# Routed expert layers gathered from group 0 alone, with later pairs shifted, a scatter signalled bank by bank, and another evacuation order in the attentions

## What is computed

```python
def hier_moe(h, w_grp, b_grp, w_exp, b_exp, w_gate, w_up, w_down):   # 4 groups of 8 experts, hidden 256
    pg = softmax(t @ w_grp + b_grp);  p_top, grp = lax.top_k(pg, 1)
    le_sel = (einsum('td,gde->tge', t, w_exp) + b_exp)[arange(T), grp[:, 0]]
    val, idx = lax.top_k(le_sel, 2)
    wts = softmax(val) * p_top
    ...
    a = silu(einsum('td,edh->teh', t, w_gate)) * einsum('td,edh->teh', t, w_up)
    y = sum over experts of (a * combine) @ w_down
```

## Time and profile before

| | |
|---|---|
| runs | 2247.03, 2251.01, 2254.46 (median 2251.01) |
| profiled execution | 2245.17, of which the span is 2243.4 |
| TensorE matmul busy | 1813.4 (81%), 13243 instructions |
| VectorE, ScalarE busy | 431.5 (19%), 396.5 (18%) |
| chain that ended last | PE 57%, DMA 33%, DVE 4%, ACT 2% |
| transfers | 716.11 MB, mean 319 GB/s |

### The profile page before, as it was taken

One profiled execution on the slowest core, in us unless ns is written; L12 is line 12 of the kernel. 1 busy time (PEld: TensorE's weight loads), 2 busy tenths in 40 slices (PEclk: granted clock), 3 DMA queues, 4 the chain that ended last, 5 costly groups with the idle time before them and its releaser, 6 DMA issues.

```text
span 2243.4 us, 30956 instructions
## 1 busy us (share of the span) xinstructions
PE 1813.4 (81%) x13243; PEld 1125.3 (50%) x13243; DVE 431.5 (19%) x1014; ACT 396.5 (18%) x898; POOL 0.6 (0%) x5
## 2 busy tenths in 40 slices
PE   7989899999898998899987556566789976656556
PEld 5858565568676655587754122211577542212113
DVE  2242211123533111223311000000244210000001
ACT  3030211122532111222321000000213310000001
POOL 0000000000000000000000000000000000000000
PEclk9999899999799999999998887877999987777778
DMA  9876799975536999933579999999942799999993
GB/s 358 255 256 251 290 389 392 392 230 185 210 152 236 360 398 397 346 125 130 187 298 413 421 422 421 421 422 421 346 141 101 298 414 421 421 421 421 421 421 163
DMA packets 184735, 716.11 MB, mean 319 GB/s; under 512 B 28396, under 2 KB 95896, under 8 KB 114072
## 3 DMA queue, kind: packets, MB, share of 16 engines
q1 hardware_dynamic: 183884, 713.61, 81.5%
q10 hardware_dynamic: 716, 0.53, 0.1%
HBM read 826.30 MB, written 1.05 MB: 369 GB/s over the span
## 4 chain that ended last, share of the span: by engine, by line
PE 57%; DMA 33%; DVE 4%; ACT 2%; SPq 2%; issue 1%; ACTq 0%; POOLq 0%; DVEq 0%
DMA ring<-in_w 27%; PE ps L986 19%; PE ps L1416 7%; PE ps L1339 7%; DMA ring<-in_moe_w_up 6%; PE ps L1349 3%; PE ps L1428 3%; PE ps L1366 2%; PE ps L1323 2%; PE ps L963 2%; PE ps L1140 2%; SPq L808 1%; PE ps L1000 1%; PE ps L1053 1%; PE ps L1041 1%
## 5 line engine op out<-in xcount | busy, mean ns | idle before, releaser
L1416 PE MATMUL ps<-ring,ptb 128*32 128x512 f32 x1936 | 316.8, 804 | 201.5 <-DMA ring<-in_w 188.0
L1416 PEld LDWEIGHTS ps<-ring,ptb 128*32 128x32 f32 x1936 | 83.5, 141 | 422.4 <-issue 407.3
L1428 PE MATMUL ps<-ring,pb 128*32 128x512 f32 x1024 | 155.3, 765 | 88.0 <-DMA ring<-in_w 85.3
L986 PE MATMUL ps<-xT,ring 128*128 128x256 f32 (+2 forms) x640 | 146.7, 388 | 1.0 <-ACT xT L1720 0.4
L1428 PEld LDWEIGHTS ps<-ring,pb 128*32 128x32 f32 x1024 | 40.8, 136 | 195.8 <-issue 191.8
L986 PEld LDWEIGHTS ps<-xT,ring 128*128 128x128 f32 (+2 forms) x640 | 117.7, 187 | 29.4 <-issue 8.4
L986 PE MATMUL ps<-oT,ring 128*128 128x256 f32 x512 | 114.0, 381 | 2.0 <-DVE oT L2228 1.1
L2457 DVE TENSOR_TENSOR kT<-pb,ps 128x1024 f32<-128x1024 f32 x8 | 9.8, 1221 | 531.6 <-ACT pb L1894 531.6
L986 PE MATMUL ps<-hT,ring 128*128 128x256 f32 x480 | 106.7, 380 | 1.5 <-ACT hT L1720 1.5
L1339 PE MATMUL ps<-ring,vt 128*32 128x256 f32 x1536 | 93.5, 400 | 16.1 <-DMA ring<-in_moe_w_up 15.6
L986 PEld LDWEIGHTS ps<-oT,ring 128*128 128x128 f32 x512 | 96.2, 190 | 15.6 <-DVE oT L2228 2.0
(11 more groups left out here) (437 smaller groups left out, 1955.2 us busy)
## 6 DMA issues: line engine op xcount, KB each, us to landing
ring<-in_w SPq DMA_DIRECT2D x370, 1024.0 KB
ring<-in_moe_w_gate SPq DMA_DIRECT2D x96, 1024.0 KB
ring<-in_moe_w_up SPq DMA_DIRECT2D x96, 1024.0 KB
ring<-in_moe_w_down SPq DMA_DIRECT2D x96, 1024.0 KB
ring<-in_ada_w SPq DMA_DIRECT2D x48, 1024.0 KB
ring<-in_diff_w_in SPq DMA_DIRECT2D x12, 1024.0 KB
ring<-in_w_o SPq DMA_DIRECT2D x8, 1024.0 KB
ring<-in_ple_gate_w SPq DMA_DIRECT2D x8, 1024.0 KB
```

The lines of the kernel that those rows point to most:

```text
L986: last = mmul(o, l, r, start=start, stop=stop)
L1416: last = mmul(ps[32 * j:32 * j + 32, 2 * a + h, :], xg[:, k, 32 * j:32 * j + 32], w[j][2 * k2 + h], start=(k == 0), stop=(k == C - 1))
L1428: last = mmul(ps[32 * j:32 * j + 32, 6 + h, :], hidT2[:, c, 32 * j:32 * j + 32], w[j][2 * c2 + h], start=(c == 0), stop=(c == C - 1))
```

## The change

Group 0 is gathered alone. `dispatch_first` builds a 128-column matrix `D0` (kept in `st`), `gather_first` gathers group 0 with 32 instructions of 128 columns into one bank for each half, and `gathered_first` evacuates them. Pairs are then groups 1 and 2, 3 and 4, and so on; the sixth is group 11 alone with 128 slots. The first half of pair 0 is gathered in group 0 into banks 4 and 5 behind the small matmuls for the combine rows; group g also gathers one half for each g up to 10. The dispatch of pair 0 no longer waits for a gather, the others move from odd to even groups. The last scatter signals after each bank, and VectorE waits bank by bank. In the attentions ScalarE's `after` runs one step later, behind the `move` of that step, and VectorE's `outputs(i - 2)` comes ahead of `neg_max(i + 2)`.

```diff
+        D0 = st[:, :].rearrange("p (a n) -> p a n", a=TT)
+        E1_PAIRS = E1_GROUPS // 2
+        E1_HALVES = 2 + 2 * E1_PAIRS
+        E1_DISPATCHES = 1 + E1_PAIRS
+        def pair_slots(p):
+            return 2 * P if p < E1_PAIRS - 1 else P
         def e1_gather_at(g):
-            return g + 2 if g + 2 < E1_HALVES else None
+            p = (g + 1) // 2
+            return (p, (g + 1) % 2) if p < E1_PAIRS else None
...
+                def gather_first(half, bank):
+                    for k in range(4 * half, 4 * half + 4):
+                        for tt in range(TT):
+                            last = mmul(ps[:, bank, P * (k % 4):P * (k % 4) + P], h_tokk[:, tt, k, :],
+                                        D0[:, tt, :], start=(tt == 0), stop=(tt == 1))
+                    last.then_inc(S("e1_xg_mm"), 1)
                 def gate_up(g):
-                    xs = xpair[g // 2 % 2]
-                    s0 = P * (1 - g if g < 2 else g % 2)
-                    pe.wait_ge(S("e1_xg_ready"), x0 + (1 if g == 0 else min(g + 2, E1_HALVES)))
+                    xs = xpair[(g - 1) // 2 % 2 if g else 1]
+                    s0 = P * ((g - 1) % 2) if g else 0
+                    pe.wait_ge(S("e1_xg_ready"), x0 + (min(g + 3, E1_HALVES) if g else 1))
...
                 def scatter(g):
...
+                            if g == E1_GROUPS - 1 and c % 2:
+                                last.then_inc(S("e1_y_mm"), 1)
...
-                gather_half(0, 0)
-                gather_half(1, 6)
+                gather_first(0, 0)
+                gather_first(1, 6)
                 for g in range(E1_GROUPS):
                     gate_up(g)
                     if g == 0:
...
                         last.then_inc(S("lr_mm"), 1)
+                        gather_half(0, 0, 4)
                     if g:
                         scatter(g - 1)
                     hidden_T(g)
                     if (at := e1_gather_at(g)) is not None:
-                        if at % 2 == 0:
-                            pe.wait_ge(S("e1_D"), E1_GROUPS // 2 * m + at // 2 + 1)
-                        gather_half(at % 2, 0)
+                        gather_half(*at, 0)
                     down(g)
-                scatter(E1_GROUPS - 1).then_inc(S("e1_y_mm"), 1)
+                scatter(E1_GROUPS - 1)
...
@@ ScalarE, attention @@
-                    if i >= 2:
-                        after(i - 2)
+                    if i >= 3:
+                        after(i - 3)
                 move(xs[-1])
+                after(len(xs) - 3)
                 after(len(xs) - 2)
                 after(len(xs) - 1)
...
@@ ScalarE, experts1: group 0 @@
                         func(sqb[:, :], psf(2, 2), ACT.Copy).then_inc(S("lr_ready"), 1)
+                        gathered(0, 0, 4)
...
@@ VectorE, attention @@
                     normalise(x)
+                    if i >= 2:
+                        outputs(xs[i - 2])
                     if i + 2 < len(xs):
                         neg_max(xs[i + 2])
-                    if i >= 2:
-                        outputs(xs[i - 2])
...
@@ VectorE, route1 @@
                 link(V.tensor_reduce(Lw[:, 0:2, :], rt_oh, AX, ALU.add))
+                dispatch_first()
                 link(V.tensor_tensor(Lp[:, :, :, :].rearrange("p b a n -> p (b a) n"),
...
-                dispatch1(0)
...
@@ VectorE, experts1 @@
-                dve.wait_ge(S("e1_xg_mm"), x0 + 2)
-                dispatch1(1)
+                dispatch1(0)
...
-                    if g % 2 and g // 2 + 2 < E1_GROUPS // 2:
-                        dve.wait_ge(S("e1_xg_mm"), x0 + g + 3)
-                        dispatch1(g // 2 + 2)
-                dve.wait_ge(S("e1_y_mm"), m + 1)
+                    if g % 2 == 0 and g // 2 + 1 < E1_PAIRS:
+                        dve.wait_ge(S("e1_xg_mm"), x0 + g + 4)
+                        dispatch1(g // 2 + 1)
                 for c in range(C):
+                    if c % 2 == 0:
+                        dve.wait_ge(S("e1_y_mm"), 4 * m + c // 2 + 1)
```

More of the change, by code:

```diff
@@ L104, in shape_constants @@
     fixed = BLK * (E1_AWAY + i // BLK) + i % BLK
-    put("slots", np.broadcast_to(np.concatenate([lane - BLK, lane, fixed]).astype(np.float32), (P, 3 * P)))
+    put("slots", np.broadcast_to(np.concatenate([lane, lane + BLK, fixed]).astype(np.float32), (P, 3 * P)))
     g = np.arange(E1_GROUPS)
@@ L1318, in slot_of, with gather_half @@
                     return ring[:, (n0 + 12 * g + s) % RING, :]
-                def gather_half(half, bank):
+                def gather_first(half, bank):
                     for k in range(4 * half, 4 * half + 4):
                         for tt in range(TT):
-                            last = mmul(ps[:, bank + k % 4 // 2, T * (k % 2):T * (k % 2) + T], h_tokk[:, tt, k, :],
-                                        Dp[:, tt, :], start=(tt == 0), stop=(tt == 1))
+                            last = mmul(ps[:, bank, P * (k % 4):P * (k % 4) + P], h_tokk[:, tt, k, :],
+                                        D0[:, tt, :], start=(tt == 0), stop=(tt == 1))
+                    last.then_inc(S("e1_xg_mm"), 1)
+                def gather_half(p, half, bank):
+                    if half == 0:
+                        pe.wait_ge(S("e1_D"), E1_DISPATCHES * m + p + 2)
+                    n = pair_slots(p)
+                    for k in range(4 * half, 4 * half + 4):
+                        for tt in range(TT):
+                            last = mmul(ps[:, bank + k % 4 // 2, T * (k % 2):T * (k % 2) + n], h_tokk[:, tt, k, :],
+                                        Dp[:, tt, 0:n], start=(tt == 0), stop=(tt == 1))
                     last.then_inc(S("e1_xg_mm"), 1)
                 def gate_up(g):
-                    xs = xpair[g // 2 % 2]
-                    s0 = P * (1 - g if g < 2 else g % 2)
-                    pe.wait_ge(S("e1_xg_ready"), x0 + (1 if g == 0 else min(g + 2, E1_HALVES)))
+                    xs = xpair[(g - 1) // 2 % 2 if g else 1]
+                    s0 = P * ((g - 1) % 2) if g else 0
+                    pe.wait_ge(S("e1_xg_ready"), x0 + (min(g + 3, E1_HALVES) if g else 1))
                     for a in range(2):
@@ L1351, in scatter @@
                                         stop=(g == E1_GROUPS - 1 and c % 2 == 1), skip_group_check=True)
-                    return last
+                            if g == E1_GROUPS - 1 and c % 2:
+                                last.then_inc(S("e1_y_mm"), 1)
                 def hidden_T(g):
@@ L1848, in experts1, with gathered_first, gathered @@
                 n0, ff, x0 = slot_moe[m], E1_FF, E1_HALVES * m
-                def gathered(at, bank):
-                    act.wait_ge(S("e1_xg_mm"), x0 + at + 1)
+                def gathered_first(half, bank):
+                    act.wait_ge(S("e1_xg_mm"), x0 + half + 1)
                     for c in range(4):
-                        k = 4 * (at % 2) + c
-                        by, add = gathered_gain(m, k)
-                        last = func(xpair[at // 2 % 2][:, k, :], ps[:, bank + c // 2, T * (c % 2):T * (c % 2) + T],
+                        by, add = gathered_gain(m, 4 * half + c)
+                        last = func(xpair[1][:, 4 * half + c, 0:P], ps[:, bank, P * c:P * c + P],
                                     ACT.Identity, scale=by, bias=add)
                     last.then_inc(S("e1_xg_ready"), 1)
-                gathered(0, 0)
-                gathered(1, 6)
+                def gathered(p, half, bank):
+                    act.wait_ge(S("e1_xg_mm"), x0 + 2 * p + half + 3)
+                    n = pair_slots(p)
+                    for c in range(4):
+                        k = 4 * half + c
+                        by, add = gathered_gain(m, k)
+                        last = func(xpair[p % 2][:, k, 0:n], ps[:, bank + c // 2, T * (c % 2):T * (c % 2) + n],
+                                    ACT.Identity, scale=by, bias=add)
+                    last.then_inc(S("e1_xg_ready"), 1)
+                gathered_first(0, 0)
+                gathered_first(1, 6)
                 for g in range(E1_GROUPS):
@@ L1866, in experts1 @@
                         func(sqb[:, :], psf(2, 2), ACT.Copy).then_inc(S("lr_ready"), 1)
+                        gathered(0, 0, 4)
                     if (at := e1_gather_at(g)) is not None:
-                        gathered(at, 0)
+                        gathered(*at, 0)
                     act.wait_ge(S("slot_used"), n0 + 12 * g + 12)
@@ L2372, in dispatch1, with dispatch_first @@
             def dispatch1(pair):
-                slots = K("slots")[:, 0:2 * P] if pair else K("slots")[:, P:3 * P]
+                n = pair_slots(pair)
+                slots = K("slots")[:, 0:n]
                 for tt in range(TT):
-                    link(V.tensor_scalar(Dp[:, tt, :], slots, Lp[:, 0, tt, pair:pair + 1], None, ALU.is_equal))
-                    last = V.scalar_tensor_tensor(Dp[:, tt, :], slots, Lp[:, 1, tt, pair:pair + 1], Dp[:, tt, :],
```

(9 more changed lines are left out.)

3 lines of the change are left out of this document (1 added, 2 removed).

## The result

The changed kernel takes 2228.4 us (median of 4 runs, 2224.5 to 2229.6), the kernel before 2249.2 (median of 4, 2247.0 to 2254.5). The ratio is 0.9907, 95% interval 0.9891 to 0.9923: 20.8 us less, between 17 and 25. The prediction was 2232.9, 18.1 less than a median of 2251.0. The profiled execution took 2228.89 with a span of 2227.1, and that of the kernel before 2243.4, so the spans differ by 16.3.

The account below looks back on a forecast made before the run. TensorE was taken to bound attentions and projections, TensorE and transfers alternately the routed layers, transfers the big expert layers' later part. 3.7 + 3.6 + 0.2 + 8.6 - 1.25 + 3.2 = 18.1 off 2251.0 gave 2232.9 us; 8-in-10 range 2223 to 2244.

Parts of the forecast that it names:

- `diff`: Attention `diff`: the wait for VectorE's copy goes, three ada steps 1.25 closer, ScalarE's row late next; 3.7 us saved.
- `nsa`: Attention `nsa`: three waits for the copy save 0.85 each, three copies ahead of transposes 0.34 each; 3.6 us saved.
- `gqa`: Attention `gqa`: four copies change places with a maximum on VectorE; 0.2 us saved, between -1.4 and 1.4.
- Last scatter: End of both routed layers: updates and squares run under the scatter, bank by bank; 2 x 1.6 = 3.2 us saved.
- The gather itself: Start of a routed layer: 32 narrow instructions take 3.9 instead of 7.07, so gate_up starts 3.3 us earlier.
- Start of the routed layers and groups 9 and 10: Both routed layers: group 1 loses its w_up wait and slow half, 8.6 us saved; groups 9 and 10 cost 1.25.
- the transfer queues have gaps later, so the later waits move along: Routed layers after group 1: later waits shift too, so the full 4.3 us is kept in each layer.
- the prediction's own bound for full queues: Routed layers: were the queues full from group 1 to the last wait, 2 x 3.3 us instead of 8.6.
- group 10's wait: Layer 1, group 10: its 2.83 us wait for w_up takes back group 9's gain; 1.45 us lost.
- Rival A: Routed layers: `down(0)` decides, queues run dry once, group 1's wait returns and 8.6 us is lost; 2241.5, chance 0.15.
- Rival C: Routed layers: shifted waits put TensorE at half clock in one half of every group; slower, 2257 us, chance 0.04.
- The base: Whole kernel before: 2251.0 us, the median of three runs, from which the sum of 18.1 was subtracted.

Follow-up runs that it names:

- light and heavy pairs: The kernel before and the changed kernel, each with half of every up matrix loaded from group 1 (2213.1, 2199.1 us) or with no transfer skipped (2468.0, 2441.7).
- split kernel: The changed kernel with ScalarE's part undone and, from group 1, half the previous group's scatter between gate_up's halves: 2219.0 us, ratio to before 0.9864.

## Why the prediction came out near

The sum was 18.1. The stages of all kernels give 17.7 (each mean over three to six kernels), the medians 20.8 (17 to 25). That the sum came within 0.4 of the stages is in part luck: the routed term was 2.35 too high, and the four others together were 2.0 too low.

- **`diff`, 3.7 forecast, 4.5 found** (old order 49.1 in the mean of five kernels, new 44.7 of five). The mechanism was right: the copy's wait gone, the row late next, the end of the stage later (last values 5.08 behind the last ada part instead of 4.72, forecast 0.4). Too small was the step: 1.37 each, not 1.25, since values start 0.33 behind the transposes' start, not 0.42, and the row costs 0.20, not 0.23. The rest is within the 1.9 that the clock moves this stage by. What was not seen is that the part which makes the row late, ScalarE's, buys nothing: the prediction costed the two parts as one edit.
- **`nsa`, 3.6 forecast, 4.1 found** (124.4 to 120.3). Ada parts 15.88 apart, not 17.13: 1.25 for a block of four steps, forecast 1.19.
- **`gqa`, 0.2 forecast, 0.5 found** (scores to the second layer's dispatch: 78.9 to 78.4), with VectorE's part alone too.
- **Last scatter, 3.2 forecast, 3.6 to 3.8 found.** The sums start 1.79 sooner: the wait of 1.63 is gone, since the squares now start from the first bank, and the projection starts another 0.1 sooner.
- **The gather itself, 3.9 forecast, 3.73 found,** 117 ns for a narrow instruction at full clock, so that gate_up of group 0 ends 3.7 sooner after the gather's start (14.48 to 10.77) and not 3.3. The rule weighed there (the Trainium skill, "TensorE: Matmul & The Clock Gate", Back-to-back issue gap) would have given 2.6, and the trace disagrees with it for this float32 form.
- **Start of the routed layers and groups 9 and 10, 8.6 - 1.25 = 7.35 forecast, 5.0 found.** This is the term that was wrong, and by parts it is 4.3 + 0.2 = 4.5 forecast and 4.0 found in layer 0, and 4.3 - 1.45 = 2.85 forecast and 1.0 found in layer 1. The size of the miss is within what one code varies by in layer 1, so it is the traces that show what failed. The first half of the step stands: no wait and no slow half in group 1, and `down(1)` comes 5.0 sooner after the gather in both layers. What failed is "the transfer queues have gaps later, so the later waits move along". In layer 0 the gain falls to 3.6 by `down(2)`, through the 0.82 for w_gate and the 0.33 shown above: TensorE comes to group 2 5.0 earlier, while the queues start only 3.7 sooner and are full from 264 to 301 (DMA share 1.01 to 1.02), so its transfers can't come as much sooner. That is near the prediction's own bound for full queues, 2 x 3.3: with it the term would have been 6.6 - 1.25 = 5.35. In layer 1 the gain is 4.4 at `down(4)`, 2.3 at `down(5)` and lost by the end. In this pair of profiles two terms take it: group 10's wait, which takes back what group 9 saves (as forecast), and slow halves, 4 where the profile of before had 3 (its group 5 waited 3.78 and then ran 64 in 3.66; in the other four kernels with that code they took 5.01 to 6.41).
- **Rival A, 0.15,** was wrong in its mechanism and right in its direction: group 1's wait did not return in either layer, but waits of later groups took back a third of the term. The light and heavy pairs show why it can't be all or nothing.
- **Rival C** did not come: 4 and 4 slow halves after, 5 and 3 before.
- **The base.** The forecast is 4.5 above the result, and 1.8 of that is the base: 2251.0 from three runs, 2249.2 with a fourth. The sum was set against the median of the runs, 5.8 above the profiled execution. The profile of before was indeed below its like: its `diff` took 47.9 where the same code took 49.3 to 49.8 in four other kernels, its layer 1 242.5 against a mean of 244.8. Against that, part of its last stretch (the windows below, unchanged code) ran at a lower clock than in other runs:

```profile
2198.00:2238.00 40.00, 30.37 (x144) 18.06 (x144) 10.54 (x16) 7.89 (x14) 0.00 (x0) 0.80 0.22 90
```

```profile
2196.00:2236.00 40.00, 26.55 (x144) 16.35 (x144) 10.54 (x16) 9.20 (x15) 0.00 (x0) 0.89 0.24 101
```

The first row is before, the second the kernel with the scatter edit: the same 144 instructions take 30.4 at 0.80 and 26.6 at 0.89. So the span's 16.3 is too small and too large in different places, and is no better a measure than the medians.

## What to carry to other kernels

Where two engines' orders are changed together, cost each alone: here one carried the whole gain, and the other cost about 1 us at the clock at which both were seen. Work moved off the start of a stage that streams weights is worth what the transfers start earlier, not the wait that vanishes first; ask where the next wait stands. And a long wait of TensorE costs twice, in itself and in the clock behind it, so independent work belongs inside the wait even if it is only split off from what follows. Here that was worth 7.3 us more, a change that the prediction hadn't thought of.

## What was not expected of the hardware

The clock behind a wait went with how long TensorE had waited. In layer 1 of the split kernel three halves followed waits of 1.86, 1.68 and 1.84 and each ran in 3.66; in the changed kernel four followed waits of 3.79, 3.43, 3.30 and 3.94 and took 5.35, 5.35, 5.35 and 6.49, in the window above at 0.68, a mix of 2.4 and 1.2 GHz. While TensorE waited, the record still read 1.00; the fall came in the half behind it. By the Trainium skill ("TensorE: Matmul & The Clock Gate", HAM oscillation) the clock falls in transfer waits; the trace agrees for the long ones and not for these three short ones. Over the twelve kernels other than the heavy pair, 46 of the 49 halves behind a wait of 3.0 to 4.2 for weights were slow (over 4.5 us), and none of the ten behind one of 1.0 to 2.1. In between it went either way, and there are exceptions: a wait of 3.57 (layer 0 of the changed kernel) and one of 3.78 (layer 1 of before) were followed by full clock, one of 2.20 by 5.35. And two of the slow halves of layer 0 come from no long wait: the up halves of groups 2 and 4, behind the narrow router products (286.79 above, 0.33 waited and 5.30 taken), are slow in the kernel before and the changed one. What decides there stays open, for with ScalarE's part alone the up half of group 2 took 3.66.

Unchanged code also varied from kernel to kernel by 3 us or more: from the span's start to the first product of 512 columns it was 48.5 to 52.3 over 14 kernels. The projection windows above show the clock's part; some kernels, the changed one among them, also waited there for a transfer of `in_ada_w` (2.29 before its last 16 ada products).
